# Twelve low parts of an input projection move from VectorE to GpSimd, and one exponential moves ahead of a tanh

## The reference, cut to what matters

```python
def hybrid_mixer(...):
    h = jnp.concatenate([h_ctx, h_lat], axis=1)
    p = (h @ w_in).astype(f32)                     # the input projection
    qkv_a, z, ab, rq, rk, rv, rg = jnp.split(p, splits, axis=-1)
    ...                                            # short_conv and silu of q, k, v; decays from ab
    q = l2_normalize(q) * (HEAD_DIM ** -0.5)
    k = l2_normalize(k)
    o_gdn = rms_norm_2(o_f + o_b, gdn_norm_g) * jax.nn.silu(z...)   # gated delta rule, both directions
    rq = apply_rope(rq...); rk = apply_rope(rk...) * (HEAD_DIM ** -0.5)
    o_ret = head_group_norm(r_f + r_b, ret_norm_g) * jax.nn.silu(rg...)  # retention, both directions
```

## Time and profile before

| | |
|---|---|
| median of the runs | 1337.15 us |
| profiled execution, span | 1335.4 us |
| TensorE busy | 1264.9 us (95%) |
| VectorE busy | 913.2 us (68%) |
| ScalarE busy | 695.0 us (52%) |
| GpSimd busy | 77.0 us (6%) |
| input projection's last part, 950.0 to 1001.5 us | TensorE 39.53, VectorE 48.08, GpSimd 3.79 us busy |

### The profile page before, as it was taken

One profiled execution on the slowest core, in us unless ns is written; L12 is line 12 of the kernel. 1 busy time (PEld: TensorE's weight loads), 2 busy tenths in 40 slices (PEclk: granted clock), 3 DMA queues, 4 the chain that ended last, 5 costly groups with the idle time before them and its releaser, 6 DMA issues.

```text
span 1335.4 us, 19244 instructions
## 1 busy us (share of the span) xinstructions
PE 1264.9 (95%) x7760; PEld 1080.7 (81%) x7760; DVE 913.2 (68%) x1429; ACT 695.0 (52%) x1132; POOL 77.0 (6%) x126
## 2 busy tenths in 40 slices
PE   7999999999999999999999999999979889899997
PEld 5899988877888887987888876786758876788885
DVE  4464553447888857687888876755796886766665
ACT  5454544446666645766666755334332444455553
POOL 1000000001000001001000001022011301000000
PEclk9999999999999999999999999999989899899999
DMA  9844335556555557257555557212533006555551
GB/s 336 327 172 145 127 126 190 189 186 241 192 189 192 186 200 265 93 190 291 189 190 189 189 189 266 72 64 103 165 124 101 2 1 212 200 189 191 191 200 48
DMA packets 31718, 230.74 MB, mean 173 GB/s; under 512 B 11000, under 2 KB 14704, under 8 KB 18704
## 3 DMA queue, kind: packets, MB, share of 16 engines
q1 hardware_dynamic: 25568, 218.14, 45.3%
q10 hardware_dynamic: 5056, 7.73, 1.6%
q0 software_dynamic: 1008, 3.67, 0.7%
HBM read 225.82 MB, written 3.71 MB: 172 GB/s over the span
## 4 chain that ended last, share of the span: by engine, by line
PE 78%; DVE 12%; ACT 6%; issue 2%; DMA 1%; POOL 1%; SPq 0%; DVEq 0%; POOLq 0%; ACTq 0%
PE ps L436 18%; PE ps L620 16%; PE ps L499 10%; PE ps L440 9%; PE ps L208 8%; PE ps L488 5%; PE ps L587 4%; DVE parts L344 3%; PE ps L559 3%; PE ps L531 2%; ACT parts L340 2%; DMA ring<-in_W 1%; DVE arena L1655 1%; DVE row L1908 1%; DVE arena L1906 1%
## 5 line engine op out<-in xcount | busy, mean ns | idle before, releaser
L344 DVE TENSOR_TENSOR parts<-ring,parts 128x1024 fp32r<-128x1024 f32 x354 | 431.4, 1224 | 278.5 <-ACT parts L340 201.0
L340 ACT ACTIVATE parts<-ring 128x1024 fp32r<-128x1024 f32 x354 | 372.7, 1057 | 296.6 <-PE ps L440 102.6
L436 PE MATMUL ps<-hall,parts 128*128 128x512 f32 x1120 | 395.1, 398 | 5.5 <-DVE hall L293 3.7
L440 PE MATMUL ps<-hall,parts 128*128 128x256 f32 x1120 | 313.8, 280 | 0.0
L620 PE MATMUL ps<-parts 128*128 128x512 f32 x1128 | 262.0, 391 | 8.6 <-DVE parts L375 8.3
L436 PEld LDWEIGHTS ps<-hall,parts 128*128 128x128 f32 x1120 | 211.1, 188 | 58.4 <-issue 3.3
L620 PEld LDWEIGHTS ps<-parts 128*128 128x128 f32 x1128 | 210.0, 188 | 57.9 <-DVE parts L375 12.6
L440 PEld LDWEIGHTS ps<-hall,parts 128*128 128x128 f32 x1120 | 212.3, 190 | 0.0
L499 PE MATMUL ps<-hall,parts 128*128 128x256 f32 x1152 | 140.7, 284 | 0.0
L499 PEld LDWEIGHTS ps<-hall,parts 128*128 128x128 f32 x1152 | 139.0, 192 | 0.6 <-DVE parts L344 0.5
L208 PE MATMUL ps<-arena 128*128 128x128 f32 (+4 forms) x934 | 111.7, 285 | 16.4 <-DMA arena<-in_onehot 6.5
(11 more groups left out here) (213 smaller groups left out, 1066.0 us busy)
## 6 DMA issues: line engine op xcount, KB each, us to landing
ring<-in_W SPq DMA_DIRECT2D x100, 2048.0 KB, 8.3
arena<-distance_tables SPq DMA_DIRECT2D x8, 384.0 KB, 8.0
gains<-in_gains POOLq DMA_DIRECT2D x5, 512.0 KB, 8.1
ring<-in_W SPq DMA_DIRECT2D x4, 512.0 KB, 9.1
arena<-in_gate_w ACTq DMA_DIRECT2D x1, 2048.0 KB, 10.6
matrices<-arena ACTq DMA_DIRECT2D x8, 256.0 KB, 2.3
x<-in_x SPq DMA_DIRECT2D x2, 512.0 KB, 5.3
gates<-in_ada_gate_b POOLq DMA_DIRECT2D x2, 512.0 KB, 6.3
```

Source lines behind the costliest of these rows:

```text
L340: return nc.scalar.activation(unit_weights(n, 0, weights), weights, ACT.Copy)
L344: return nc.vector.tensor_tensor(unit_weights(n, 1, weights), weights, unit_weights(n, 0, weights), ALU.subtract)
L436: last = nc.tensor.matmul(ps[:, b, :].rearrange("p (a b) -> p a b", a=2), w[:, 0, :], hparts[:, :, k, :], start=k == 0, stop=False)
L440: last = nc.tensor.matmul(ps[:, b, 0:S], w[:, 1, :], hparts[:, 0, k, :], start=False, stop=k == KT - 1)
```

## The change

Twelve units, z 0 to rg 3 (20 to 31), get their low parts from GpSimd's `tensor_tensor` instead of VectorE's, counted on a semaphore of their own; TensorE's waits choose the semaphore by unit. In GpSimd's queue units 20 to 25 stand ahead of the lengths of the queries and units 26 to 31 behind them. VectorE's calls of `low_parts` skip these units. The exponential EX is issued behind the tap of convolution 5 and ahead of its tanh and of the copies of the turned keys.

```diff
--- before.py
+++ after.py
@@ -364,9 +364,13 @@
                 last.then_inc(S_("high_parts"), 1)
             units_split["high"] = max(units_split["high"], end)
 
+        by_pool = set()
+
         def low_parts(dve, end):
 
             for n in range(units_split["low"], end):
+                if n in by_pool:
+                    continue
                 _, weights, inputs, _ = UNITS[n]
                 dve.wait_ge(S_("high_parts"), n + 1)
                 if n not in ahead:
@@ -376,6 +380,21 @@
                 last.then_inc(S_("low_parts"), 1)
             units_split["low"] = max(units_split["low"], end)
 
+        def low_parts_pool(pool, units):
+
+            for n in units:
+                assert n in by_pool and UNITS[n][2] is None
+                weights = UNITS[n][1]
+                pool.wait_ge(S_("high_parts"), n + 1)
+                nc.gpsimd.tensor_tensor(unit_weights(n, 1, weights), weights, unit_weights(n, 0, weights), ALU.subtract).then_inc(S_("low_parts_pool"), 1)
+
+        def low_ready(pe, n):
+
+            if n in by_pool:
+                pe.wait_ge(S_("low_parts_pool"), sum(m <= n for m in by_pool))
+            else:
+                pe.wait_ge(S_("low_parts"), sum(m not in by_pool for m in range(n + 1)))
+
         def unit_weights(n, part, like):
 
             w = parts[:, n % NPARTS, part, 0:D]
@@ -428,7 +447,7 @@
                     for n in range(4):
                         u = self.first + 4 * j + n
                         b = self.bank(j) + n
-                        pe.wait_ge(S_("low_parts"), u + 1)
+                        low_ready(pe, u)
                         for k in range(KT):
                             if j == 0 and n == 0:
                                 norm.column_done(pe, k)
...
@@ -892,6 +911,7 @@
         n_ffn2 = Norm(6, 22, x, xn, hT, lambda k: modc[:, 16 + k:17 + k], lambda k: modT[:, 24 + k, 0:1], r_mix2.x_ready, shifted_before=2, paired=True)
 
         u0 = w_k.first
+        by_pool.update(range(w_z.first, w_rg.first + 4))
 
         ORDER = attention_order()
         proj = [c for c in ORDER if c[0] in "VK"]
@@ -1045,8 +1065,10 @@
                 if n >= 2:
                     pool.wait_ge(S_("diff"), n - 1)
                 decay_in(n % 2, n // 2 % TT2, n // (2 * TT2))
+            low_parts_pool(pool, range(w_z.first, w_rq.first + 2))
             for i in range(TT2, TT2 + TT):
                 inverse_length(i)
+            low_parts_pool(pool, range(w_rq.first + 2, w_rg.first + 4))
             pool.wait_ge(S_("EX"), 1)
             pool.wait_ge(S_("tok_vector"), TT2)
             w_rg.done(pool)
@@ -1365,12 +1387,13 @@
             for i in range(4, 8):
                 high_parts(act, u0 + 8 + i)
                 conv_taps(i)
+                if i == 5:
+                    act.wait_ge(S_("sums"), 1)
+                    nc_a.activation(EX[:, :, :, :].rearrange("p a b c -> p (a b c)"), ps[:, SUMS_BANK, 0:320], ACT.Exp).then_inc(S_("EX"), 1)
                 conv_tanh(i)
                 if i == 5:
                     for t in range(TT2):
                         turned("knT", t)
-                    act.wait_ge(S_("sums"), 1)
-                    nc_a.activation(EX[:, :, :, :].rearrange("p a b c -> p (a b c)"), ps[:, SUMS_BANK, 0:320], ACT.Exp).then_inc(S_("EX"), 1)
             for n in range(4):
                 decay(n)
             high_parts(act, u0 + 16)
```

More of the change, by code:

```diff
@@ L628, in unit @@
             def unit(self, pe, kk):
-                pe.wait_ge(S_("low_parts"), self.first + kk + 1)
+                low_ready(pe, self.first + kk)
                 self.products(kk, 0, kk % 4 == 3)
```

## The result

The changed kernel takes 1350.49 us (median of six runs, 1344.52 to 1351.81) against 1337.89 us of the kernel before in the same series (1332.72 to 1342.08). The ratio is 1.008, with a 95% interval of 1.0058 to 1.0103: slower by 10.7 us, between 7.8 and 13.8 (the two medians themselves lie 12.6 us apart). The profiled execution has a span of 1347.2 us against 1335.4. The prediction had said 1342.5 with a range up to 1348, so the direction of its sum was right and its size too small, and the time lies outside the range.

The account below looks back on a forecast made before the run. VectorE's queue was taken to bound the stretch up to the query transposes. -2.8 (exponentials) - 9.1 (low parts gone) + 17.3 (shut out) = +5.4 us gave a span of 1340.8, plus 1.75 for the median: 1342.5 us, range 1334 to 1348.

Parts of the forecast that it names:

- What bounds the stretch: From 950 us to the query transposes at 1000.14 us, VectorE's own queue was said to set the time.
- Part 1: EX ahead of the tanh removes TensorE's 2.85 us stall at value unit 3; VectorE's bound stretch starts 2.8 us earlier.
- the third difference's wait: The third decay difference, waiting for the first decay's exponential, was named as next late, limiting the gain to 2.7 to 2.8 us.
- VectorE's loss of eight low parts: Units 20 to 27, ahead of the query normalisation, leave VectorE's queue: 8 x 1.14 = 9.1 us gained.
- The exclusion: GpSimd and VectorE instructions reading SBUF shut each other out, for the GpSimd instruction less about 0.13 us; 17.3 us added net.
- the eight units that the sum priced at 1.91: Low parts of units 22 to 27, 29 and 30, beside elimination or a silu product: 1.91 us each, 15.3 us.
- the three that it called mostly covered: Units 20, 21 and 28, beside convolution, rotation and gating that read PSUM: 0.34 + 0.44 + 0.95 = 1.7 us.
- Rival B: Same exclusion with a longer GpSimd instruction, both inputs being full streams; slower by over 0.5%, from 2.2 us on; chance 0.36.
- part 2: Twelve low parts moved to GpSimd: VectorE's queue loses 9.1 us and gains 17.3 us up to the query transposes.
- this clock costs no more: TensorE idles some 11 us ahead of the query transposes; the clock's fall behind that costs no more than behind 3.12 us.
- The median's offset: The median was taken to lie 1.75 us above the profiled span, turning 1340.8 into 1342.5 us.
- the prediction's three places: Trace rows at 891.92, 1050.83 and 1051.83 us, read as VectorE and GpSimd shutting each other out.

Follow-up runs that it names:

- e6: The kernel before with the exponential EX moved ahead of the tanh and all elimination steps but the last left out; 1317.94 us.
- e8: The kernel before with EX moved ahead and VectorE's order changed: elimination in smaller pieces, query normalisation ahead of step 14; 1332.09 us, ratio 0.9948.
- e1: The kernel before with only the exponential EX moved ahead of the tanh, VectorE keeping all low parts; 1335.72 us, ratio 0.9983.
- e9: The changed kernel with GpSimd's twelve subtractions replaced by zero fills about as long, so GpSimd writes but does not read; 1331.61 us.
- e4: The kernel before with twelve extra pairs of GpSimd fills into scratch that nobody waits for, plus three GpSimd sizes measured earlier; 1340.10 us.
- e2: The changed kernel with EX back behind the tanh, so only the twelve low parts move to GpSimd; 1347.98 us, ratio 1.0078.
- e3: The kernel before with twelve extra GpSimd subtractions of 128x1024 into scratch that nobody waits for; VectorE keeps its low parts; 1361.34 us.
- e10: The kernel of e8, with its changed VectorE order, plus the changed kernel's twelve low parts on GpSimd; 1332.66 us.

## Why the prediction was wrong

- **What bounds the stretch** held: VectorE's queue up to the query normalisation. e6 (-16.3 us of the middle without the elimination) and e8 (-12.2 by order alone) show it.
- **Part 1, 2.8 us** held in size where the clock stayed up: e1's head is 2.48 us shorter than before's, and the prediction named the third difference's wait, 1.99 us in the traces. What the sum left out is what that wait does to TensorE: in after the clock fell behind it, and the head is only 0.78 us shorter. The earlier trace rows had shown such a fall behind 2.85 us; the prediction gave back its 1.54 us and did not ask whether the new wait would take it again.
- **VectorE's loss of eight low parts, 9.1 us**, held: without the reads VectorE reaches the normalisation 9.0 us earlier (e9).
- **The exclusion** held as a mechanism, and its size failed: this is the step that broke. The sum had 15.3 + 1.7 = 17.0 us; 20.7 were shut out, and e9 against after gives 20.8 at the normalisation. The main term that failed is the length of a GpSimd low part. The prediction took 2.04 us, "the row with the same number of elements", less 0.13, as 1.91 us for each VectorE instruction shut out. A low part measured 2.44 in after, and each instruction fully held was longer by 2.0 to 2.2. Of the 3.7 us missing, 1.5 are in the eight units that the sum priced at 1.91 (16.8 instead of 15.3). The other 2.3 are in the three that it called mostly covered (4.0 instead of 1.7), nearly all at unit 21, whose low part started at 953.15, 0.05 us ahead of a silu product that then took 2.64. Whether a shorter low part of unit 20 would have let that product pass first no run shows. The row behind 2.04 is a product with a factor repeated along the row; e4 has 1.94 us for such a product and 2.39 for the subtraction of two full inputs at 1024 columns. Rival B named the second full input, gave 7.7 at 2.3 us, and was given 0.36 where the forecast had 0.38. The Trainium skill, "GPSIMD Engine Reference", section 3.1, has the figure from which the prediction's estimate was 2.3 us. That was nearer than the row: the measurement is 2.39 alone and 2.44 in the kernel, so the estimate is a little low here.
- **The sum again with the measured terms**: head -0.8; middle -9.1 + 20.7 = +11.6 (e2 measured +11.55); in after the low clock behind the wait of 12.09 costs 1.1 us more than in e2 behind the same wait (the 16 products behind the query transposes took 3.62 us at a granted clock of 0.50, and 2.53 at 0.74 in e2), which makes 12.7, against 12.4 measured; tail +0.3. Together +12.0, and the span grew by 11.8. The 17.3 - 9.1 = 8.2 of the prediction's part 2 lacks 3.4 us, part 1 lacks 2.0, and the low clock behind the long wait 1.1. The prediction had held that this clock costs no more than the one behind before's 3.12 us: from the transposes to unit 28 after needs 5.04 us, before 4.43, and e2 4.05.
- **The median's offset** of 1.75 us above the span held for the profiled execution alone (1348.96 us at a span of 1347.2). The median of the six runs lies 3.3 us above that span, so of the 8.0 us between 1342.5 and 1350.49 some 6.4 are the sum's and 1.5 this offset's.
- **The rule on the port**: by the Trainium skill, "SBUF — State Buffer", section "Who interferes with whom", VectorE with two SBUF inputs contends with a GpSimd instruction that reads SBUF, and not with one that only writes it. The runs agree on both halves: reads 17.8 us of the middle in e3, writes none in e4 (70.78 against 70.80). One of the prediction's three places, the 8 columns at 1050.83, has a single SBUF input, as e4's 40 columns have, so it goes beyond what that sentence states.
- **The range** ended at 1348 because it left out "instructions over about 2.4 us". The measured 2.44 lay just past that edge, and neither the clock's 2 us nor the median's 1.5 were in a bound.

What stays open: why the clock falls behind the same 1.99 us wait in some executions and not in others, and whether the second full input or the subtraction makes a GpSimd low part longer than the products of the earlier trace rows.

## What to carry to other kernels

Before work goes to GpSimd beside a VectorE queue that sets the time, count the VectorE instructions with SBUF inputs that would run beside it: each GpSimd instruction that reads SBUF and meets one of them costs that queue most of its own length (2.0 to 2.2 of 2.44 us here), however short the instruction that it meets, so giving away 1.14 us for 2.1 loses. Price an unseen instruction by a row with the same operation and the same kind of inputs, not by the same number of elements, and where removing one stall leaves another of about 2 us, add the clock's fall behind it to the sum. A gain can also lie in the order: moving steps that nobody waits for behind one that TensorE waits for took 12 us out of this stretch, of which half came back as the next wait.

## What the runs showed of the hardware that was not expected

- A GpSimd `tensor_tensor` of 128x1024 takes 2.39 us as a subtraction of two full inputs and 1.94 as a product with one input repeated (e4); fills take 0.95 and held nobody up.
- The exclusion also holds for a VectorE instruction with one SBUF input: 2.27 us for 128x40 at 874.48 in e4, where its neighbours of the same size take 0.18 to 0.20.
- Identical streams of products, with TensorE busy all the time at a granted clock of 1.00, ran at two paces in different executions. In 620 to 740 us, long ahead of the change, before and then after have (columns: length, busy PE and count of products, granted clock, DMA share, GB/s):

```profile
620.00:740.00 120.00, 120.00 (x682) 1.00 0.53 190
...
620.00:740.00 120.00, 120.00 (x694) 1.00 0.55 197
```

  12 products more in 120 us is 1.8%, some 2 us. The starts agree with the counts: from the product at 616.33 to the one at 790.45 before needs 174.12 us, and after for the same ones (615.94 to 787.71) 171.77. Of the thirteen profiled kernels after, e2, e9 and e10 had 694, the others 681 or 682. These 2.35 us are most of the 2.7 by which after's value unit 2 starts earlier than before's although nothing ahead of it was changed, and a reason why single spans are not compared here to better than some 3 us. Its cause is open.
